# Three layers of a mixed model on one core: where the activations lie in SBUF, modulo 256 bytes

## The chip, the cores and the metric

The kernel runs on one core of one Trainium2 chip. The metric is the device time of one execution, in microseconds, first to last instruction with what lies around it; lower is better. Before the change it is 1613.02 us, the median of 3 runs.

## The reference

256 tokens of width 1024, float32, go through three layers. What matters here is that nearly all the work is products of the activations with large weight matrices, each weight used once:

```python
for layer in range(2):
    x = x + 0.5 * swiglu(rmsnorm(x, ffn1_norm[layer]), ffn1_w_gu[layer], ffn1_w_down[layer])   # 1024 -> 2 x 2816 -> 1024
    h = rmsnorm(x, mix_norm[layer])
    y = gated_deltanet(h, ...) if layer == 0 else sliding_window_attention(h, ...)
    x = x + y
    x = x + 0.5 * swiglu(rmsnorm(x, ffn2_norm[layer]), ffn2_w_gu[layer], ffn2_w_down[layer])
x = rmsnorm(x, final_norm)
# second block: one layer
proj = rms_norm(x, norm_mix) @ w_in             # attention, RWKV-7 in both directions, and gates
merged = gates_0 * (attn @ w_up_attn) + gates_1 * (rw @ w_up_rwkv)
x = x + merged @ w_out
x = x + square(relu(rms_norm(x, norm_ffn) @ w_ff1)) @ w_ff2          # 1024 -> 4096 -> 1024
x = x + (p @ w_ple) * sigmoid(rms_norm(x, norm_ple) @ w_ple_gate)
```

## The kernel before

**Weights.** All weights are cut into 225 pieces of 128 partitions by 2048 float32 (8192 bytes in each partition, 1 MB in all). There are four slots (`SLOTS`). SyncE loads piece p into `raw` with two transfers of 512 KB as soon as TensorE has used piece p - 4 (semaphore `piece_used`, L2380 to L2394). ScalarE rounds it to `w_hi` in the 32-bit matmul type F32R (L2715), VectorE writes the rest, `raw - w_hi`, over it as `w_lo` (L2888). `lo_ready` then releases the matmuls of the piece.

**Dense matmuls.** Activations are held transposed and split in the same way (`h_hi`/`h_lo` behind a norm, `g_hi`/`g_lo` behind a gate, and so on). `three()` (L2516) makes each product out of three matmuls, hi by hi, lo by hi and hi by lo; its lines are L2518, L2519 and L2520. In each the weight block of 128 x 128 is the stationary operand (a weight load, 512 bytes in each partition) and 256 tokens of the activation are the moving one (1024 bytes). Narrow jobs (L2523 on) run over chunks of 512 output columns and read `h`; wide jobs (L2572 on) run over the inner dimension and read `g`, `o`, `ao`, `mg`, `rw` or `p`. A piece is 16 such products, 48 matmuls. TensorE's queue is these in a fixed order; where a stage begins it waits for `h_ready`, which VectorE gives with `h_lo` (L2963).

**The gate logits.** In the first mixer, L637 to L639 do the same three matmuls 8 times over with `ba_hi`/`ba_lo` as weights. These are not in a slot but lie behind `h`.

**Addresses.** `Map.take` lays one tile behind the other and rounds each to 32 bytes. The map `fixed` begins at byte 16512 of each partition. The starts that matter, with their remainder modulo 256:

| tiles | start | modulo 256 |
|---|---|---|
| `w_hi`, `raw`/`w_lo` (four slots of 8192 each) | 16512, 49280 | 128 |
| `xT`, `cst` | 82048, 90240 | 128 |
| `p_hi`, `p_lo`, `sq`, `rstd`, `full3` | from 102464 | 64 |
| `h_hi`, `h_lo` | 122688, 130880 | 64 |
| the arena behind: `g_hi`, `g_lo`, `ba_hi`, `ba_lo`, `o_hi`, `ao_hi_b`, `mg_hi`, `rw_hi` and their partners | from 139072 | 64 |

Blocks of weights are 512 bytes apart and rows of activations 1024, so every operand of a dense matmul has the remainder of its tile. `y_tok`, the output, is laid from the end of SBUF down.

Of the kernel before, what the change touches and what calls it, by code (L numbers as in the profile page):

```python
# [195 lines left out]
def build(nc, A, out, stop=None):  # L196
    base = -(-16481 // 32) * 32
    fixed = Map(nc, base, 229344)
# [14 lines left out]
    sq = fixed.take("sq", [P, KD, T])  # L213
    rstd = fixed.take("rstd", [P, T])
    full3 = fixed.take("full3", [P, 3, 2, T])
    h_at = fixed.at
    h_hi = fixed.take("h_hi", [P, KD, T], F32R)
    h_lo = fixed.take("h_lo", [P, KD, T], F32R)
# [2900 lines left out]
```

## Time and profile before

| | us |
|---|---|
| median of 3 runs | 1613.02 |
| lowest, highest | 1601.33, 1614.93 |
| the profiled execution | 1607.01 |
| its span | 1605.0 |
| TensorE busy in it | 1536.2 (96%) |
| VectorE, ScalarE, GpSimd busy | 1064.6, 730.3, 69.9 |
| mean granted clock of TensorE | 0.989 |

All times of the trace are from this one execution, and sums are made against its 1607.01. The start-to-start distance of two matmuls that follow each other is shorter than the duration that the profile gives for one, since they overlap; where the text speaks of a beat it means that distance. The granted clock is a share of 2.4 GHz; it is 1.00 or 0.50.

### The profile page before, as it was taken

The page shows a single profiled execution, that of the slowest core. Times are in us where ns is not written, and L with a number is a line of the kernel's source. Part 1 is how long each engine was busy: PE and PEld are TensorE (multiplying, and loading weights), DVE is VectorE, ACT ScalarE, POOL GpSimd, SP SyncE. Part 2 cuts the span into 40 slices and gives each one's busy share as a digit, 9 for nine tenths or more (in the row PEclk, how much of TensorE's full clock was granted, in tenths as well). Part 3 has the DMA queues.
Part 4 walks back from the last instruction along what each step waited for, and adds up shares of the span by engine and source line. Part 5 has one row for each costly group of instructions (what it writes and reads, how often), then busy time and mean ns, then how long its engine had stood idle before and what let it go on. Part 6 is the DMA issues. An engine that isn't in the chain of part 4 may idle for free. (4 is left out here: it accounts for less than half of the span.)

```text
span 1605.0 us, 36127 instructions
## 1 busy us (share of the span) xinstructions
PE 1536.2 (96%) x15669; PEld 1478.2 (92%) x15669; DVE 1064.6 (66%) x1277; ACT 730.3 (46%) x814; POOL 69.9 (4%) x52
## 2 busy tenths in 40 slices
PE   7999989999999999999998999999997889999998
PEld 6999989878999999999988999999886778999997
DVE  5766487764867547664677766467768776777436
ACT  5443345543534344433446433354565444555333
POOL 2000000100100001000101000021000000100000
PEclk9999999999999999999999999999999999999999
DMA  8665545201556556555533555564320012555552
GB/s 269 189 192 201 185 157 169 96 2 51 183 188 193 200 184 184 183 184 187 181 131 96 182 187 191 185 201 145 120 79 3 3 56 81 184 184 189 202 186 79
DMA packets 155065, 243.26 MB, mean 152 GB/s; under 512 B 9283, under 2 KB 106174, under 8 KB 154814
## 3 DMA queue, kind: packets, MB, share of 16 engines
q1 hardware_dynamic: 154510, 240.63, 45.7%
q8 instruction: 102, 1.67, 0.4%
q10 hardware_dynamic: 432, 0.79, 0.2%
q14 instruction: 21, 0.17, 0.0%
HBM read 240.34 MB, written 1.05 MB: 150 GB/s over the span
## 5 line engine op out<-in xcount | busy, mean ns | idle before, releaser
L2888 DVE TENSOR_TENSOR w_lo<-raw,w_hi 128x2048 fp32r<-128x2048 f32 x225 | 522.9, 2335 | 243.0 <-ACT w_hi L2715 242.1
L2518 PE MATMUL dense_ps<-h_hi,w_hi 128*128 128x256 f32 x2368 | 668.3, 282 | 12.2 <-DVE h_lo L2963 8.6
L2519 PE MATMUL dense_ps<-h_lo,w_hi 128*128 128x256 f32 x2368 | 662.0, 280 | 0.0
L2520 PE MATMUL dense_ps<-h_hi,w_lo 128*128 128x256 f32 x2368 | 662.0, 280 | 0.0
L2715 ACT ACTIVATE w_hi<-raw 128x2048 fp32r<-128x2048 f32 x225 | 428.5, 1913 | 332.6 <-DMA raw<-in_ffn_w_down 116.2
L2518 PEld LDWEIGHTS dense_ps<-h_hi,w_hi 128*128 128x128 f32 x2368 | 450.5, 190 | 18.3 <-issue 17.8
L2519 PEld LDWEIGHTS dense_ps<-h_lo,w_hi 128*128 128x128 f32 x2368 | 447.4, 189 | 0.8 <-issue 0.5
L2520 PEld LDWEIGHTS dense_ps<-h_hi,w_lo 128*128 128x128 f32 x2368 | 448.1, 189 | 0.0
L2520 PE MATMUL dense_ps<-g_hi,w_lo 128*128 128x256 f32 x960 | 266.9, 278 | 0.0
L2518 PE MATMUL dense_ps<-g_hi,w_hi 128*128 128x256 f32 x960 | 266.9, 278 | 0.0
L2519 PE MATMUL dense_ps<-g_lo,w_hi 128*128 128x256 f32 x960 | 266.9, 278 | 0.0
L2518 PEld LDWEIGHTS dense_ps<-g_hi,w_hi 128*128 128x128 f32 x960 | 181.7, 189 | 0.0
L2520 PEld LDWEIGHTS dense_ps<-g_hi,w_lo 128*128 128x128 f32 x960 | 180.2, 188 | 0.0
L2519 PEld LDWEIGHTS dense_ps<-g_lo,w_hi 128*128 128x128 f32 x960 | 180.2, 188 | 0.0
L2843 ACT ACTIVATE act<-act 128x512 f32<-128x512 f32 x44 | 27.8, 632 | 178.4 <-DVE act L3055 178.4
L3055 DVE TENSOR_TENSOR act<-dense_ps,rstd 128x512 f32<-128x512 f32 x44 | 30.4, 691 | 58.2 <-PE dense_ps L2520 54.7
L2683 POOL TENSOR_TENSOR sq<-sq 128x512 f32<-128x512 f32 x14 | 20.1, 1438 | 924.0 <-ACT sq L2786 924.0
L2954 DVE TENSOR_TENSOR g_lo<-full,g_hi 128x512 f32 (+1 forms) x60 | 41.5, 692 | 4.9
L595 ACT ACTIVATE ly_r<-mixer_ps 128x512 f32<-128x512 f32 x48 | 26.5, 594 | 23.7 <-PE mixer_ps L538 18.0
L3059 DVE TENSOR_TENSOR full<-act,full 128x512 f32<-128x512 f32 x44 | 31.5, 716 | 8.7 <-ACT act L2843 4.8
L3006 DVE SCALAR_TENSOR_TENSOR xT<-dense_ps,xT 128x1024 f32<-128x1024 f32 x14 | 17.1, 1221 | 30.2 <-PE dense_ps L2520 30.2
L981 DVE SCALAR_TENSOR_TENSOR qkv<-dense_ps,cols,qkv 128x255 f32<-128x255 f32 (+2 forms) x72 | 29.7, 475 | 11.1 <-ACT qkv L836 10.7
(554 smaller groups left out, 1750.5 us busy)
## 6 DMA issues: line engine op xcount, KB each, us to landing
raw<-in_ffn_w_gu SPq DMA_DIRECT2D x176, 512.0 KB, 4.6
raw<-in_ffn_w_down SPq DMA_DIRECT2D x88, 512.0 KB, 4.1
raw<-in_w_ff SPq DMA_DIRECT2D x64, 512.0 KB, 4.2
raw<-in_w_in SPq DMA_DIRECT2D x36, 512.0 KB, 4.4
raw<-in_a_w_in SPq DMA_DIRECT2D x32, 512.0 KB, 4.3
raw<-in_a_w_out SPq DMA_DIRECT2D x8, 512.0 KB, 4.0
raw<-in_b_w_in SPq DMA_DIRECT2D x8, 512.0 KB, 4.2
raw<-in_b_w_out SPq DMA_DIRECT2D x8, 512.0 KB, 4.1
```

What stands on the lines that cost most here:

```text
L595: act.activation(y[:, 4 * half:4 * half + 4, :], bank_pair(half), ACT.Copy).then_inc(y_kept, 1)
L981: last = dve.scalar_tensor_tensor(out=o_, in0=ps, scalar=cols[:, at_:at_ + 1], in1=o_, op0=ALU.mult, op1=ALU.add)
L2518: pe.matmul(o, hi, mh, start=start, stop=False)
L2519: pe.matmul(o, hi, ml, start=False, stop=False)
L2520: return pe.matmul(o, lo, mh, start=False, stop=stop)
L2683: pool.tensor_tensor(src[:, k:k + 2, :], src[:, k:k + 2, :], src[:, k + 2:k + 4, :], ALU.add).then_inc(sq_folded, 1)
L2715: act.activation(w_hi[:, p % SLOTS, :], raw[:, p % SLOTS, :], ACT.Copy).then_inc(hi_ready, 1)
L2843: act.activation(act2[:, q, :, :], act2[:, q, :, :], ACT.Silu).then_inc(act_ready, 1)
L2888: dve.tensor_tensor(w_lo[:, p % SLOTS, :], raw[:, p % SLOTS, :], w_hi[:, p % SLOTS, :].bitcast(F32), ALU.subtract).then_inc(lo_ready, 1)
L2954: return dve.tensor_tensor(lo, full, hi.bitcast(F32), ALU.subtract)
L3055: dve.tensor_tensor(act2[:, q, :, :], lower, by_rms(2), ALU.mult).then_inc(gate_scaled, 1)
L3059: link(dve.tensor_tensor(full2[:, q, :, :], act2[:, q, :, :], full2[:, q, :, :], ALU.mult))
```

## The change

In front of `h_hi` 192 bytes are left free. `h_hi` and `h_lo` begin at 122880 and 131072 then, the arena at 139264; all of them have the remainder 0 modulo 256, the weight slots still 128. The tiles ahead of `h_hi` stay, and so does `y_tok`. All else is the same.

```diff
     rstd = fixed.take("rstd", [P, T])
     full3 = fixed.take("full3", [P, 3, 2, T])
+    fixed.at += 192
     h_at = fixed.at
     h_hi = fixed.take("h_hi", [P, KD, T], F32R)
     h_lo = fixed.take("h_lo", [P, KD, T], F32R)
     arena = fixed.at
```

## Rows read from the trace of the kernel before

**Rows 1.** The page, part 1: busy us, share of the span and instructions

```profile
PE 1536.2 (96%) x15669; PEld 1478.2 (92%) x15669; DVE 1064.6 (66%) x1277; ACT 730.3 (46%) x814; POOL 69.9 (4%) x52
```

**Rows 2.** The page, part 5: line, form and count, busy and mean, idle before

```profile
L2888 DVE TENSOR_TENSOR w_lo<-raw,w_hi 128x2048 fp32r<-128x2048 f32 x225 | 522.9, 2335 | 243.0 <-ACT w_hi L2715 242.1
L2518 PE MATMUL dense_ps<-h_hi,w_hi 128*128 128x256 f32 x2368 | 668.3, 282 | 12.2 <-DVE h_lo L2963 8.6
...
L2715 ACT ACTIVATE w_hi<-raw 128x2048 fp32r<-128x2048 f32 x225 | 428.5, 1913 | 332.6 <-DMA raw<-in_ffn_w_down 116.2
```

**Rows 3.** Table of stretches: width, each engine's busy us (count), clock, DMA

```profile
41.00:198.00 157.00, 157.00 (x1388) 157.00 (x1387) 99.44 (x86) 61.01 (x40) 0.00 (x0) 1.00 0.59 193
427.00:594.00 167.00, 167.00 (x1476) 167.00 (x1475) 103.25 (x87) 67.18 (x46) 0.00 (x0) 1.00 0.60 195
1402.00:1566.00 164.00, 164.00 (x1449) 164.00 (x1449) 96.59 (x80) 77.42 (x65) 0.00 (x0) 1.00 0.56 193
597.00:783.00 186.00, 186.00 (x1579) 185.90 (x1577) 114.81 (x95) 76.99 (x58) 6.29 (x4) 1.00 0.58 186
886.00:1060.00 174.00, 174.00 (x1479) 174.00 (x1479) 103.47 (x87) 67.65 (x47) 0.00 (x0) 1.00 0.58 187
```

**Rows 4.** Groups by line, TensorE and its weight loads, 427 to 594 us

```profile
L2518 PE MATMUL dense_ps<-h_hi,w_hi 128*128 128x256 f32 x318 | 87.8, 276 | 0.0
...
L2518 PEld LDWEIGHTS dense_ps<-h_hi,w_hi 128*128 128x128 f32 x317 | 59.5, 188 | 0.0
```

**Rows 5.** The same groups, 597 to 783 us

```profile
L2519 PE MATMUL dense_ps<-h_lo,w_hi 128*128 128x256 f32 x349 | 98.1, 281 | 0.0
...
L2518 PEld LDWEIGHTS dense_ps<-h_hi,w_hi 128*128 128x128 f32 x348 | 66.7, 192 | 0.0
```

**Rows 6.** Timeline of TensorE: start us, us, instruction, idle before it

```profile
595.59 0.36 PE L2518 MATMUL dense_ps<-h_hi,w_hi 128*128 128x256 f32 x1 [0.63 <-DVE h_lo L2963]
595.78 0.28 PE L2519 MATMUL dense_ps<-h_lo,w_hi 128*128 128x256 f32 x1
...
596.49 0.28 PE L2519 MATMUL dense_ps<-h_lo,w_hi 128*128 128x256 f32 x1
```

**Rows 7.** The same timeline, up to the first gate logit, and the last

```profile
240.97 0.28 PE L2519 MATMUL dense_ps<-h_lo,w_hi 128*128 128x256 f32 x1
...
241.54 0.28 PE L637 MATMUL mixer_ps<-h_hi,ba_hi 128*128 128x256 f32 x1
...
244.30 0.28 PE L639 MATMUL mixer_ps<-h_hi,ba_lo 128*128 128x256 f32 x1
```

**Rows 8.** The tile `mixer_ps`, 241 to 245 us: durations ns min/median/max, first and last start

```profile
L637 PEld LDWEIGHTS mixer_ps<-h_hi,ba_hi x8: 188/192/192, 241.4 to 243.9; 128*128 128x128 f32 x8
L637 PE MATMUL mixer_ps<-h_hi,ba_hi x8: 283/283/284, 241.5 to 244.1; 128*128 128x256 f32 x8
```

**Rows 9.** Line L2519 in 198 to 427 us and in 1060 to 1200 us

```profile
L2519 PE MATMUL dense_ps<-h_lo,w_hi x291: 275/276/420, 207.3 to 427.0; 128*128 128x256 f32 x146
...
L2519 PE MATMUL dense_ps<-h_lo,w_hi x288: 276/281/416, 1061.5 to 1198.9; 128*128 128x256 f32 x144
```

**Rows 10.** Table of stretches, 16 to 19 us

```profile
16.00:19.00 3.00, 3.00 (x16) 3.00 (x15) 2.68 (x3) 3.00 (x7) 0.00 (x0) 0.50 1.11 350
```

**Rows 11.** Timeline of TensorE there, first and last of six

```profile
16.92 0.41 PE L2518 MATMUL dense_ps<-h_hi,w_hi 128*128 128x256 f32 x1
...
17.99 0.41 PE L2520 MATMUL dense_ps<-h_hi,w_lo 128*128 128x256 f32 x1
```

**Rows 12.** Timeline of TensorE, eight matmuls of `ones` by `sq`

```profile
199.20 1.89 PE L2627 MATMUL mixer_ps<-sq,cst 128*128 128x256 f32 x8
```

**Rows 13.** Timeline of the weight loads behind the pause of rows 6

```profile
595.56 0.19 PEld L2518 LDWEIGHTS dense_ps<-h_hi,w_hi 128*128 128x128 f32 x1 [0.80 <-issue]
595.67 0.19 PEld L2519 LDWEIGHTS dense_ps<-h_lo,w_hi 128*128 128x128 f32 x1
```

**Rows 14.** The page, part 6: transfers, KB each, median us to landing

```profile
raw<-in_ffn_w_gu SPq DMA_DIRECT2D x176, 512.0 KB, 4.6
```

## The prediction

> **What bounds the kernel now.** I read the page first. Its table of busy times gives TensorE 96% of the span, VectorE 66% and ScalarE 46% [rows 1]. The costliest groups are the three lines of `three()` and the splits that feed them [rows 2]. So the rate of the dense matmuls sets the time, if they run without gaps. The table of stretches says so: in five long stretches TensorE and its weight loads are busy all the time, at a granted clock of 1.00 (2.4 GHz), VectorE about 60% of it [rows 3].
>
> The same table holds the point of this case. A window counts every matmul that touches it, and one lasts 276 or 281 ns, so some 2.4 of each count began before the window. From 427 to 594 us that is 1476 - 2.4 in 167 us, a beat (start to start) of 113.3 ns; from 886 to 1060 us it is 1479 - 2.4 in 174 us, a beat of 117.8 ns [rows 3]. Code, shapes, tiles and clock are the same in both; only the job differs. Line by line, a matmul of the first stretch lasts 276 ns and its weight load 188 ns [rows 4]; in the second they last 281 ns, and one of the three loads 192 ns [rows 5]. I call them the short and the long beat.
>
> The timeline shows that a beat is kept while the stream runs and chosen anew where it restarts. The short beat of [rows 4] ends where TensorE waits 0.63 us for `h_lo`; from 595.78 on it runs at 118 ns (0.71 us for six) [rows 6].
>
> Does the place in SBUF matter to it? The reader should look for dense matmuls whose operands lie otherwise. In all 10,800 dense matmuls (225 pieces, one split of L2888 each [rows 2], of 48) the weight piece begins 64 bytes above the moving tile, modulo 256 (128 against 64). There is one exception of the same form: the 24 matmuls of `gate_logits` (L637 to L639), where `ba_hi`/`ba_lo` and `h_hi`/`h_lo` all lie at 64, a distance of 0. They start at 241.54 without a pause, out of a stream in the short beat (0.57 us for the five beats before), and go from there to 244.30 in 23 beats, 120.0 ns each [rows 7]. Each lasts 283 ns, and nearly each of their loads 192 ns [rows 8]. So three beats are seen: 120.0 at distance 0, and 113.3 or 117.8 at distance 64.
>
> **What the change does.** No instruction, wait, transfer or byte is added or removed. `h_hi` and all behind it move up 192 bytes, from 64 to 0 modulo 256; weight slots, `xT`, constants, `sq`, `rstd`, `full3` and `p_hi`/`p_lo` stay. For 10,752 of the 10,800 dense matmuls (all but the 48 of `ple`, which read `p_hi`/`p_lo`) the distance goes from 64 to 128. The 24 of `gate_logits` keep distance 0.
>
> **What each part costs.** *The mix of beats now.* The three stretches in the short beat hold 1388 + 1476 + 1449 = 4,313 matmuls, the two in the long one 1579 + 1479 = 3,058 [rows 3]. The other 3,430 lie in stretches where both occur. In these the median of L2519 is 276 ns from 198 to 427 us and 281 ns from 1060 to 1200 us [rows 9], so I take half of each. That makes 4,770 in the long beat and 5,980 of the moved ones in the short.
>
> *If distance 128 always gives the short beat*, 4,770 x 4.5 ns = 21.5 us go.
>
> *The other bounds.* Distance 128 has no row in a stream of this form, so I take the nearest from both sides. Above: the long beat everywhere costs 5,980 x 4.5 = 27 us; the 120.0 ns of distance 0 costs 5,980 x 6.7 + 4,770 x 2.2 = 51 us. Below: at the granted clock of 0.50 (1.2 GHz) [rows 10] the same matmuls take 1.07 us for five beats, 214 ns each, so 107 ns at 2.4 GHz is the stream alone [rows 11]. Eight matmuls of `ones` by `sq`, which take two such passes each, start (1.89 - 0.38)/7 = 215.7 ns apart, 2.4 more than twice 106.7 [rows 12]. So no beat should be below some 109 ns; 10,752 x 4.1 = 44 us under the short beat. A load is near that too: 595.56 to 595.67, 110 ns, for two loads before the stream has formed [rows 13]. I take the short beat: it is a steady state that rows show, and the load leaves little below it.
>
> *Does the rest keep up?* A piece is 48 matmuls, 5.44 us in the short beat. In the short stretch from 427 to 594 us VectorE is busy for 103.25 of 167 us and ScalarE for 67.18; TensorE has no gap at all [rows 3]. A freed slot is refilled in 4.6 us [rows 14], then split in 1.9 by ScalarE and 2.3 by VectorE [rows 2], 8.8 in all, against 16.3 us that the three other pieces last. Of the two states the faster is already fed, so a saved beat is saved time; at the floor below VectorE's share would go from 62% to 64%.
>
> *Other accesses that move against each other.* The small matmuls of the mixers also read moved against unmoved tiles, but most restart every few instructions and wait for VectorE or ScalarE. VectorE's `h_lo` reads `xT` and `h_hi`, whose distance changes too; TensorE waits 8.6 us for it in all [rows 2], and if it slowed by as much as the beats differ, 4%, that is 0.3 us. Both at nothing, up to 2 us either way for the range.
>
> **Sum.** The profiled execution took 1607.0 us (span 1605.0 and 2.0 around it). 1607.0 - 21.5 = 1585.5. The median of the runs is 1613.0, six above it, and they spread from 1601 to 1615. I hold the choice at restarts for the cause of that spread: 6 us are 1,300 beats of 4.5 ns. A kernel with one beat would not have it, so I add nothing.
>
> A rule speaks against all of this. The Trainium skill ("SBUF — State Buffer", section Who interferes with whom) says that TensorE and ScalarE never wait on anyone, and "TensorE: Matmul & The Clock Gate", Step-by-step: what each phase is for, that the two read ports are independent, so loading the next weights takes no bandwidth from the running matmul. By these the distance is nothing, and the time stays 1607. The rows of `gate_logits` speak against it, as one place of 24 matmuls, which also differ in adding to one PSUM tile all along.
>
> **The rivals.**
> - *The distance decides nothing, or both beats remain.* For it: the beat is a matter of how the stream restarts, and distance 64 already gives both. The moving operand reads 1024 bytes in a beat and the weights 512, so it laps them twice in a ring of 256 whatever the distance; the change only moves the places from 1/8 and 5/8 of a beat to 1/4 and 3/4. Against: the switch at 241.54 without a pause. Time: 1607, and by the runs 1601 to 1615.
> - *The other side: the long beat always.* If a catch further inside a beat is what can't be absorbed, every restart falls into it. It decides by its share: with 4,770 + 6/0.0045 = 6,100 of the 10,752 in the long beat (57%) the kernel stands at the median of 1613, and from 9,700 (90%) it is slower by over 1%. Time: 1607 + 27 = 1634.
> - *As bad as distance 0*, if what matters is a ring of 128 bytes: 128 is then 0. For it: one row shows 0 to be bad, and none shows how long the ring is. Time: 1607 + 51 = 1658.
> - *Better than the short beat*: the 6.6 ns that it has above the stream alone are themselves a collision that the new distance avoids. Time down to 1585 - 44 = 1541. Against: the load's 110 ns.
>
> **How the numbers follow.** Distance 0 costs most and 64 less; 128 is the farthest in a ring of 256, so the short beat is likeliest: 0.45, 1585 us, its own range 1575 to 1595. Better than it 0.08; no effect or both beats 0.24; the long beat 0.13; as distance 0 0.10. The range 1560 to 1640 leaves out 0.10 above and most of 0.08 below. A measurement here can tell about 1% of 1613 from no change: faster (under 1597) 0.45 + 0.08 = 0.53, within 0.24, slower 0.13 + 0.10 = 0.23.
>
> **What would show it.** Right: in the table of stretches every long stretch at 113.3 ns; L2518 to L2520 at 276 ns and loads at 188 in all jobs; 24 matmuls of `gate_logits` still 283 ns; no new gap of TensorE. Wrong: 281 ns and 192 ns where 276 and 188 stood; or a duration that is none of these; or `gate_logits` changed though its distance isn't. If the beat shortens and the span doesn't, TensorE must show waits for `w_lo`, and the paragraph on keeping up was wrong.

## The result and the profile after

The kernel got slower. The median of four runs is 1643.1 us (1640.6 to 1644.2), beside it that of the kernel before 1607.2 us (1601.0 to 1614.9). The ratio is 1.0219, with a 95% interval of 1.0159 to 1.0278. The forecast was 1585, its range 1560 to 1640.

The profiled execution took 1642.43 us (span 1640.5), 35.4 more than that of before. First the page of the kernel after, busy times and costliest groups (all lines stand one further down than before):

```profile
PE 1571.0 (96%) x15669; PEld 1513.3 (92%) x15669; DVE 1064.4 (65%) x1277; ACT 730.0 (44%) x814; POOL 69.7 (4%) x52
...
L2519 PE MATMUL dense_ps<-h_hi,w_hi 128*128 128x256 f32 x2368 | 676.6, 286 | 11.4 <-DVE h_lo L2964 7.8
L2889 DVE TENSOR_TENSOR w_lo<-raw,w_hi 128x2048 fp32r<-128x2048 f32 x225 | 522.3, 2332 | 249.8 <-ACT w_hi L2716 248.9
```

TensorE is busy 34.8 us longer than before with the same 15669 matmuls, and VectorE and ScalarE as long as before [rows 1]. The wait for `h_lo` went from 8.6 to 7.8 us and the mean `w_lo` split from 2335 to 2332 ns [rows 2]. So nothing else got slower and no wait was added: the matmuls themselves come later after each other. The table of stretches shows it, three long ones of the kernel after (columns as in [rows 3]):

```profile
43.00:205.00 162.00, 162.00 (x1367) 162.00 (x1366) 96.78 (x84) 60.65 (x39) 0.00 (x0) 1.00 0.59 186
440.00:600.00 160.00, 160.00 (x1350) 160.00 (x1350) 98.10 (x82) 60.74 (x40) 0.00 (x0) 1.00 0.57 183
625.00:800.00 175.00, 175.00 (x1474) 174.90 (x1473) 104.26 (x86) 67.25 (x45) 0.32 (x1) 1.00 0.57 182
```

Counted as in the prediction, 1350 - 2.4 in 160 us is a beat of 118.7 ns, and the other two come to 118.7 and 118.9. It is neither of the two beats of [rows 3]: 5.4 ns above the short one and 0.9 above the long one, at the same granted clock of 1.00. The groups by line of the kernel after, 440 to 600 us, give the durations:

```profile
L2521 PE MATMUL dense_ps<-h_hi,w_lo 128*128 128x256 f32 x313 | 88.1, 281 | 0.0
...
L2519 PEld LDWEIGHTS dense_ps<-h_hi,w_hi 128*128 128x128 f32 x312 | 58.7, 188 | 0.0
```

All three lines last 281 ns, and all loads 188, where [rows 4] had 276 and 188 and [rows 5] 281 and, for one load in three, 192. Taken over all dense matmuls and gate logits whose start follows the last one by 90 to 130 ns (10,635 before, 10,619 after), the mean distance of starts is 115.41 ns before and 118.71 after. (118.71 - 115.41) x 10,752 = 35.5 us, against 35.4 measured. Nor does the work of the other engines make the beat: from 450 to 540 us of the kernel after, matmuls that start while VectorE and ScalarE are both busy follow at 118.64 ns, those that start while both are idle at 118.64 too.

Distance 128 has a second beat, which the long stretches don't show. Some 440 of the moved matmuls, in four streams, follow each other at 120.0 ns. The longest of these streams begins at 220.6 us, behind a stretch at a granted clock of 0.50 (214 to 220 us), and runs up to the gate logits. Its end, 24 beats in 2.88 us:

```profile
248.83 0.28 PE L2521 MATMUL dense_ps<-h_hi,w_lo 128*128 128x256 f32 x1
...
251.71 0.28 PE L2521 MATMUL dense_ps<-h_hi,w_lo 128*128 128x256 f32 x1
251.83 0.28 PE L638 MATMUL mixer_ps<-h_hi,ba_hi 128*128 128x256 f32 x1
```

It weighs little, 440 x 1.3 ns = 0.6 us in the whole time.

A control lies in the same execution. The 48 matmuls of `ple` read `p_hi`/`p_lo`, which did not move. Timeline of TensorE in the kernel after, inside that piece:

```profile
1599.81 0.28 PE L2520 MATMUL mixer_ps<-p_lo,w_hi 128*128 128x256 f32 x1
...
1601.62 0.28 PE L2521 MATMUL mixer_ps<-p_hi,w_lo 128*128 128x256 f32 x1
```

Sixteen beats in 1.81 us, 113 ns: the short beat, in the one place where the distance is still 64. The other 24 matmuls of `ple`, behind 16 of another form, beat at 117.8, the other beat of that distance. The gate logits, whose distance stayed 0 although both their operands moved, last 283 ns as before [rows 8], in the tile `mixer_ps` of the kernel after, 246 to 254 us:

```profile
L638 PE MATMUL mixer_ps<-h_hi,ba_hi x7: 281/283/283, 251.8 to 254.0; 128*128 128x256 f32 x7
```

They are unchanged, as they should be, but they prove less: the stream ahead of them has the same 120.0 ns here.

### The profile page after: what moved, and what is told of

It is laid out like the page before. It is cut to its first block and busy times, and to the rows that moved or that the text cites. A ratio compares the mean times of both kernels' runs of the same rounds, so it can differ in the third digit from the quotient of the medians.

```text
span 1640.5 us, 36127 instructions
## 1 busy us (share of the span) xinstructions
PE 1571.0 (96%) x15669; PEld 1513.3 (92%) x15669; DVE 1064.4 (65%) x1277; ACT 730.0 (44%) x814; POOL 69.7 (4%) x52
## 5 line engine op out<-in xcount | busy, mean ns | idle before, releaser
L2519 PE MATMUL dense_ps<-h_hi,w_hi 128*128 128x256 f32 x2368 | 676.6, 286 | 11.4 <-DVE h_lo L2964 7.8
L2889 DVE TENSOR_TENSOR w_lo<-raw,w_hi 128x2048 fp32r<-128x2048 f32 x225 | 522.3, 2332 | 249.8 <-ACT w_hi L2716 248.9
L2521 PE MATMUL dense_ps<-h_hi,w_lo 128*128 128x256 f32 x2368 | 669.7, 283 | 0.0
L2520 PE MATMUL dense_ps<-h_lo,w_hi 128*128 128x256 f32 x2368 | 669.7, 283 | 0.0
L2519 PEld LDWEIGHTS dense_ps<-h_hi,w_hi 128*128 128x128 f32 x2368 | 449.6, 190 | 17.5 <-issue 17.0
L2520 PEld LDWEIGHTS dense_ps<-h_lo,w_hi 128*128 128x128 f32 x2368 | 449.7, 190 | 0.9 <-issue 0.5
L2521 PEld LDWEIGHTS dense_ps<-h_hi,w_lo 128*128 128x128 f32 x2368 | 449.2, 190 | 0.0
L2520 PE MATMUL dense_ps<-g_lo,w_hi 128*128 128x256 f32 x960 | 270.1, 281 | 0.0
L2519 PE MATMUL dense_ps<-g_hi,w_hi 128*128 128x256 f32 x960 | 270.1, 281 | 0.0
L2521 PE MATMUL dense_ps<-g_hi,w_lo 128*128 128x256 f32 x960 | 270.1, 281 | 0.0
L2520 PEld LDWEIGHTS dense_ps<-g_lo,w_hi 128*128 128x128 f32 x960 | 180.7, 188 | 0.0
L2519 PEld LDWEIGHTS dense_ps<-g_hi,w_hi 128*128 128x128 f32 x960 | 180.7, 188 | 0.0
L2521 PEld LDWEIGHTS dense_ps<-g_hi,w_lo 128*128 128x128 f32 x960 | 180.7, 188 | 0.0
```

The lines of the kernel that those rows point to most:

```text
L2519: pe.matmul(o, hi, mh, start=start, stop=False)
L2520: pe.matmul(o, hi, ml, start=False, stop=False)
L2521: return pe.matmul(o, lo, mh, start=False, stop=stop)
L2889: dve.tensor_tensor(w_lo[:, p % SLOTS, :], raw[:, p % SLOTS, :], w_hi[:, p % SLOTS, :].bitcast(F32), ALU.subtract).then_inc(lo_ready, 1)
```

## The experiments

Every kernel below computes the same with the same instructions; only places in SBUF differ. "Mean beat" is the mean distance of starts defined above, from the one profiled execution. The kernel before ran beside each group, too: 1602.8 us (median of 13) beside the e1 kernels, 1601.0 beside e2, 1605.6 beside e3, 1604.6 beside e4 and 1598.5 beside e5. A single run of a kernel at distance 64 is uncertain by 10 us either way (the 13 runs went from 1593.2 to 1613.2), so the readings of single runs rest on beats.

The theories that the expectations call A and B are: A, the beat depends on the distance between weight piece and moving tile, modulo 256; B, on where the activations themselves lie.

### Distance or place

`e1_both_moved` puts the activations where the kernel after has them, at 0 modulo 256, and takes the weights along, so that the distance is 64 again:

```diff
-    base = -(-16481 // 32) * 32
+    base = -(-16481 // 32) * 32 + 192
```

> The 192 bytes stand in front of the weight slots instead, so that weights, constants and activations all move together: the activations lie at 0 modulo 256 as in the changed kernel, but the weights 64 above them as before. Theory A: both beats of before, 113.3 and 117.8 ns, 1600 to 1615 us, and no beat of 118.7. Theory B (the activations at 0 modulo 256 are slow by themselves): 118.7 ns in all jobs, about 1643 us.

1604.1 us, median of 10 (1591.9 to 1613.2), ratio 1.0012 (0.9979 to 1.0046). In its profiled execution (1591.9) the mean beat is 114.04. Its stretch from 450 to 560 us:

```profile
450.00:560.00 110.00, 110.00 (x973) 110.00 (x972) 72.11 (x64) 43.67 (x29) 0.00 (x0) 1.00 0.59 196
```

973 - 2.4 in 110 us is the short beat, 113.3 ns; other jobs of the same execution run at 117.8. Both beats of before are back with the activations at the place of after. The distance theory holds and the place theory falls.

`e1_distance_0` and `e1_distance_192` leave the weights and use the gap of the change with another size, `fixed.at += 64` and `fixed.at += 128` in place of 192:

> The gap is 64 bytes: h_hi and all behind it lie at 128 modulo 256, as the weight pieces. Theory A: the dense matmuls do as the 24 of the gate logits did at distance 0, 120.0 ns a beat and 283 ns a matmul everywhere, 10,752 x (120.0 - 115.4) = 49 us over before, about 1656 us. Theory B: as before, 1600 to 1615.

> The gap is 128 bytes in place of 192: h_hi and all behind it lie at 192 modulo 256, the weight pieces 192 above them (or 64 below). Theory A (the beat of the dense matmuls hangs on the distance from the moving tile to the weight piece modulo 256, and on nothing else that the gap moves): one or two steady beats that no other distance has; if only the size of the distance on the ring counts, 192 is as 64, both 113.3 and 117.8 ns, about 1600 to 1615 us; if it counts which of the two is ahead, something else between 109 ns (1541 us) and 120 ns (1657 us). Theory B (the absolute place of the activations modulo 256 decides, 0 being bad): beats as before, 113.3 and 117.8.

Distance 0: 1650.8 us, mean beat 119.93. The page of that kernel, and its stretch from 450 to 560 us:

```profile
L2519 PE MATMUL dense_ps<-g_hi,w_hi 128*128 128x256 f32 x960 | 271.7, 283 | 0.0
```

```profile
450.00:560.00 110.00, 110.00 (x919) 110.00 (x918) 73.08 (x69) 41.63 (x29) 0.00 (x0) 1.00 0.55 182
```

919 - 2.4 in 110 us is 120.0 ns, and 283 ns is what the gate logits take [rows 7, 8]. The reading of 24 matmuls that the prediction leant on holds for the moved 10,752 as well: every unbroken stream of 60 or more beats at 119.8 to 120.0.

Distance 192: 1629.3 us, median of 4 (1628.7 to 1629.5), ratio 1.0170 (1.0113 to 1.0227), mean beat 117.68. Its stretches:

```profile
450.00:560.00 110.00, 110.00 (x936) 110.00 (x936) 72.23 (x66) 43.02 (x29) 0.00 (x0) 1.00 0.57 185
...
920.00:1060.00 140.00, 140.00 (x1191) 140.00 (x1190) 83.78 (x71) 52.63 (x34) 0.00 (x0) 1.00 0.55 185
```

Both are the long beat, 117.8. So a kernel that has almost only the long beat exists (its last job alone, some 190 matmuls, runs at 113.3), and its time is near what the prediction gave for that rival, 1634. Its four runs lie within 0.8 us, where the 13 beside them of the kernel before spread over 20. That fits the prediction's statement that the spread at distance 64 is the choice between the two beats.

### Half of the change

`e1_arena_only` leaves `h_hi`/`h_lo` at distance 64 and moves only what lies behind them to 128:

```diff
     h_lo = fixed.take("h_lo", [P, KD, T], F32R)
+    fixed.at += 192
     arena = fixed.at
```

> The 192 bytes stand behind h_lo: h stays at distance 64, and only g, o, ao, mg, rw (3,648 of the dense matmuls) come to distance 128. Theory A: in one run the jobs that read h have beats of 113.3 or 117.8 ns (matmuls of 276 or 281 ns) and those that read the arena 118.7 (281.4 ns), with a switch at each job's border without a pause; 3,648 x (118.7 - 115.4) = 12 us, about 1619 us. Against it: the beat is chosen at a restart and kept, so g has what h had ahead of it.

1612.0 us, mean beat 116.09. The groups by line, 450 to 560 us, hold narrow and wide jobs side by side:

```profile
L2519 PE MATMUL dense_ps<-h_hi,w_hi 128*128 128x256 f32 x255 | 70.4, 276 | 0.0
...
L2519 PE MATMUL dense_ps<-g_hi,w_hi 128*128 128x256 f32 x67 | 18.9, 281 | 0.0
```

The same line, form and weight slots give 276 ns where `h` is read, not moved, and 281 where `g` is, moved. All wide jobs of the run beat at 118.7 and all narrow ones at 113.3 or 117.8. The cost goes exactly with the tiles that move.

### How the distances lie

With another gap in front of `h_hi` (32, 96, 160 and 224 bytes) come distances 32, 224, 160 and 96. `e2_far_128` takes a gap of 448, which is 128 modulo 256 like the change, but 384 and not 128 modulo 512.

> The gap is 32 bytes: the weight pieces lie 32 above the moving tiles. Theory A in the form 'the beat changes with each 64 bytes': 32 falls between 0 (120.0 ns) and 64 (113.3 or 117.8) and does as one of them, 1650 or 1590 to 1615 us. Theory A in the form 'the beat changes gradually': a beat of its own, about 117 to 119 ns, 1620 to 1640 us.

> The gap is 224 bytes: the weight pieces lie 96 above the moving tiles, between 64 (113.3 or 117.8 ns) and 128 (118.7). By steps of 64 it does as one of the two; gradually it has a beat of its own. If one beat of 113.3 exists that every restart falls into, it is here or at 32, and the time is 1585 us.

> The gap is 96 bytes: the weight pieces lie 224 above the moving tiles, between 192 (117.8 ns) and 256 = 0 (120.0). By steps of 64: 117.8 or 120.0, 1629 or 1651 us. Gradually: between the two, about 1640 us.

> The gap is 448 bytes, 256 more than in the changed kernel: the distance is again 128 modulo 256, but 384 modulo 512 where the changed kernel has 128. Theory A with a ring of 256: beats of 118.7 ns in all jobs and 1640 to 1645 us, as the changed kernel. With a ring of 512 or more: another beat, as 384 would be a distance not tried so far.

> The gap is 160 bytes, the last distance of the ring in steps of 32: weight pieces 160 above the moving tiles, between 128 (118.7 ns) and 192 (117.8). Theory A: a beat of about 118 ns and 1630 to 1643 us, and none of 113.3, which has stood at distance 64 only.

The four `e4` kernels go finer. Tiles begin at multiples of 32 bytes, so `h_hi` and `h_lo` are taken 8 columns longer and read from inside. The cut below is the line of `h_hi` for distance 48; that of `h_lo` and the gaps that keep the rest in place are left out, and starts of 2 or 6 columns and other gaps give the other distances. Only `h` is moved; the wide jobs stay at 64 as a control.

```diff
-    h_hi = fixed.take("h_hi", [P, KD, T], F32R)
+    h_hi = fixed.take("h_hi", [P, KD * T + 8], F32R)[:, 4:4 + KD * T].rearrange("p (k t) -> p k t", t=T)
```

> h_hi and h_lo lie 48 below the weight pieces, the arena 64 as before (narrow jobs show distance 48, wide jobs 64). If the short beat belongs to a band around 64: narrow jobs at 113.3 ns, alone or beside 117.8. If to the 64-byte step alone: about 118 as at 32.

> h_hi and h_lo lie 56 below the weight pieces, the arena 64. Band: 113.3 ns in the narrow jobs, alone or beside 117.8. Single place: about 118. If the long beat is missing here: narrow jobs all at 113.3, 1590 us or less.

> h_hi and h_lo lie 72 below the weight pieces, the arena 64. Band: 113.3 ns in the narrow jobs, alone or beside 117.8. Single place: 117.3 to 120.0 as at 96. If the long beat is missing here: narrow jobs all at 113.3, 1590 us or less.

> h_hi and h_lo lie 80 below the weight pieces, the arena 64. Band: 113.3 ns in the narrow jobs, alone or beside 117.8. Single place: 117.3 to 120.0 as at 96.

All together, in the order of the distance. The last column has the beats of the moved jobs, each a mean over a stream of at least 60 matmuls without a break; in the `e4` rows these are the narrow jobs, while the mean beat beside them is over all jobs.

| distance | us | mean beat | beats of the moved jobs, ns |
|---|---|---|---|
| 0 | 1650.8 | 119.93 | 120.0 |
| 32 | 1637.7 | 118.32 | 118.3 |
| 48, `h` alone | 1622.9 | 117.22 | 119.2; 116.7 for some 450 matmuls |
| 56, `h` alone | 1637.7 | 117.99 | 120.0 to 120.5 |
| 64, before | 1607.0 | 115.41 | 113.3 or 117.8 |
| 72, `h` alone | 1631.7 | 117.93 | 120.0 |
| 80, `h` alone | 1626.2 | 117.45 | 119.3 |
| 96 | 1641.5 | 118.70 | 117.3, 118.7 or 120.0 |
| 128, the change | 1642.4 | 118.71 | 118.7; 120.0 for some 440 matmuls |
| 128 (384 modulo 512) | 1640.1 | 118.69 | 118.7; 120.0 for some 260 |
| 160 | 1652.9 | 119.95 | 120.0 |
| 192 | 1628.7 | 117.68 | 117.8; 113.3 for some 190 |
| 224 | 1622.9 | 117.23 | 116.7 or 117.8 |

The beat is no smooth function of the distance. 64 is the best of the twelve, and its neighbours 8 bytes away are as bad as 0. The stretch from 450 to 540 us, all in `h`, first of `e4_distance_72`, then of `e3_distance_160`:

```profile
450.00:540.00 90.00, 90.00 (x752) 90.00 (x752) 59.13 (x54) 33.80 (x23) 0.00 (x0) 1.00 0.59 186
```

```profile
450.00:540.00 90.00, 90.00 (x753) 90.00 (x752) 58.65 (x56) 34.55 (x24) 0.00 (x0) 1.00 0.58 181
```

752 - 2.4 and 753 - 2.4 in 90 us are 120.1 and 119.9 ns. Several expectations missed. 160 was to lie between 128 and 192 and has the beat of 0; 224 was to have 117.8, 120.0 or something between and has 116.7 beside 117.8; no band around 64 was found, and without one 48 and 56 were to be about 118. The groups by line of `e4_distance_48`, 450 to 560 us:

```profile
L2521 PE MATMUL dense_ps<-h_hi,w_hi 128*128 128x256 f32 x270 | 76.3, 283 | 0.0
...
L2521 PE MATMUL dense_ps<-g_hi,w_hi 128*128 128x256 f32 x41 | 11.3, 276 | 0.0
```

The repeat at 384 modulo 512 has the beat of the change, from 450 to 560 us in `e2_far_128` (930 - 2.4 in 110 us, 118.6):

```profile
450.00:560.00 110.00, 110.00 (x930) 110.00 (x929) 74.28 (x68) 42.71 (x29) 0.00 (x0) 1.00 0.59 187
```

So at this distance 256 more bytes change nothing but which streams fall to 120.0. That fits a ring of 256 and speaks against one of 512. So does the kernel before: modulo 512 its weight pieces lie 320 bytes above `h`, but 64 above `p`, and both jobs show 113.3 and 117.8. A ring of 128 is excluded by 0 and 128, or 64 and 192, which differ.

In the `e4` kernels a second thing differs from 64: the tiles begin off a multiple of 64. Nor do the distances 32, 96, 160 and 224 keep them on one. Perhaps such a start costs by itself. `e5_all_moved_32` adds 32 to `base`, so that distance 64 stays and every tile begins at 32 modulo 64:

> 32 more bytes in front of the weight slots: all tiles move together, the distance stays 64, but weights (160 modulo 256) and activations (96) both begin 32 behind a multiple of 64. Theory A, distance alone: 113.3 and 117.8 ns as before, 1590 to 1615 us. Theory L (a start off the multiple of 64 costs by itself, as one more line to read): about 118 ns or more, 1630 us or more.

1610.5 us, mean beat 115.23, and only the beats 113.3 and 117.8 in it:

```profile
450.00:560.00 110.00, 110.00 (x973) 110.00 (x972) 74.49 (x66) 43.52 (x30) 0.00 (x0) 1.00 0.61 194
625.00:780.00 155.00, 155.00 (x1318) 155.00 (x1318) 92.87 (x78) 56.96 (x37) 0.00 (x0) 1.00 0.58 188
```

A start off a multiple of 64 costs nothing at distance 64. Starts at 8, 16 or 24 modulo 32 were not tried at that distance; for 48 to 80 this stays possible.

### Which pair of operands

While one matmul runs, the weights of the next are loaded, so two distances could count: that between the moving tile and its own weights, or that to the weights being loaded. In the change all are the same. Four kernels move one tile of the four that `three()` reads:

```diff
# e3_w_lo_128: 64 bytes before the slots of raw/w_lo, 192 behind them
+    fixed.at += 64
     raw_at = fixed.at
# e3_h_lo_128: 192 bytes before h_lo, 64 behind it (e3_h_lo_192: 128 and 128)
+    fixed.at += 192
     h_lo = fixed.take("h_lo", [P, KD, T], F32R)
# e5_w_hi_128: base + 64, and 192 bytes between w_hi and raw
+    fixed.at += 192
     raw_at = fixed.at
```

> Only raw/w_lo moves, by 64 bytes: w_lo lies 128 above the moving tiles, w_hi 64 as before. Each dense product is h_hi by w_hi (L2518 of before), h_lo by w_hi (L2519), h_hi by w_lo (L2520), and the profile starts the load of the next matmul within 4 ns of the start of this one. Theory C (the moving operand of a matmul meets the load that runs beside it, the next one's): w_lo is loaded beside L2519, so L2519 alone is stretched. Theory O (a matmul is slowed by the place of its own weights): L2520 alone. Both: a mean beat between 113.3 and 118.7 ns, about 115 to 117, 1600 to 1625 us. Theory N (all three must agree, the mix falls in a state of its own): another beat.

> Only h_lo moves: it lies 128 below the weight pieces, h_hi and the arena 64 as before. It is the moving operand of L2519, beside which w_lo is loaded. Theories C and O both: in narrow jobs L2519 stretched as in e3_w_lo_128 by theory C, a mean beat of some 115 to 117 ns; in wide jobs 113.3 or 117.8 as before; 1600 to 1620 us. If C holds, its narrow jobs have the same pattern of beats as those of e3_w_lo_128; if O, another.

> Only h_lo moves, to distance 192; h_hi and the arena stay at 64. Theory C or O: L2519 as at distance 192, the other two as at 64, a mean beat of the narrow jobs of 115 to 118 ns (1605 to 1630 us). A mix that leaves the long beat no hold would give 113.3 always, 1585 us.

> Only w_hi moves: it lies 128 above the moving tiles, raw/w_lo 64 as before. w_hi is loaded beside L2518 and L2520 of before (2 of 3), w_lo beside L2519. Theory C (each matmul by the load beside it) or O (by its own weights): two of three matmuls as at 128, one as at 64, a mean beat no lower than that of e3_w_lo_128, 118.2, and no higher than 118.7. Theory N (the sequence as a whole falls in a steady state of its own): another beat, lower or higher than both.

| kernel | us | mean beat | beats of streams of 60 or more, ns |
|---|---|---|---|
| `w_lo` at 128 | 1633.2 | 118.23 | 118.2 or 118.3 in every job |
| `h_lo` at 128 | 1628.5 | 117.25 | narrow 118.7 to 119.0; wide 113.3 or 117.8 |
| `h_lo` at 192 | 1628.5 | 117.14 | narrow 117.8; wide both |
| `w_hi` at 128 | 1635.0 | 118.17 | 117.8, 118.7 or 120.0, by job |

If each matmul paid for its own pair, `w_lo` or `h_lo` at 128 would put one matmul in three at 118.7 and leave two at 113.3, a mean of 115.1. Measured are 118.2 and more. The page of `e3_w_lo_128`:

```profile
L2520 PE MATMUL dense_ps<-h_hi,w_hi 128*128 128x256 f32 x2368 | 676.2, 286 | 11.4 <-DVE h_lo L2965 7.9
...
L2521 PE MATMUL dense_ps<-h_lo,w_hi 128*128 128x256 f32 x2368 | 667.9, 282 | 0.0
L2522 PE MATMUL dense_ps<-h_hi,w_lo 128*128 128x256 f32 x2368 | 663.0, 280 | 0.0
```

In this kernel only L2522 has moved weights, and it is the shortest of the three. One matmul out of place shifts all three: from 450 to 540 us the starts of L2521, L2522 and L2520 follow those before them by 119.0, 119.5 and 116.2 ns, and none by 113.3. Both pairings put one matmul in three at 128 in the first two kernels and so ask for like results; the patterns differ, and no line is the dear one in all of them. By either pairing `w_hi` at 128 was to have a mean beat between 118.2 and 118.7. The mean, 118.17, lies at the edge of that, but its streams don't: most beat at 117.8 and some at 120.0. That rather fits the third theory of the expectations (N), by which the sequence as a whole falls into a state of its own. The runs settle neither pairing. They do show that a sum by parts is wrong, and that moving a third of the pairs costs most of what moving all of them costs (2.8 of the 3.3 ns for `w_lo`).

## Why the prediction was wrong

**What it had right.** What bounds the kernel, and that nothing else limits it: the time follows the beat. 1607.0 + (mean beat - 115.41) x 10,752 gives the time of every profiled execution within 6 us (distance 0: 1655.6 against 1650.8; `e1_both_moved`: 1592.3 against 1591.9). The mechanism: the distance modulo 256, not the place; the job and the restart choose only among the beats of a distance. The reading of the gate logits as a price of distance 0 was right: 120.0 ns there, 120.0 in `e1_distance_0`. "Does the rest keep up" and "other accesses at nothing" held, though a slower beat tests the first only weakly; `e1_both_moved` tests it better, with most jobs at 113.3 and 1591.9 us. The count of matmuls in the long beat was too low: with 4,770 of them there the mean would be 113.3 + 4.5 x 4,770 / 10,750 = 115.3, and it is 115.4, some 260 more, 1 us.

**The step that failed** is "I take the short beat" under *The other bounds*, and its ground in the last part: "Distance 0 costs most and 64 less; 128 is the farthest in a ring of 256". Two points, one good and one bad, were made into a slope. The runs show no slope: 8 bytes from the good place a beat is 6.7 ns longer (with the start of the tile as a second suspect), and 160 costs as much as 0. The 113.3 ns were taken for the ordinary state of the stream, to which a farther distance would return. They are the exception: usual at 64, and elsewhere held only at 192, by the last job. The term "4,770 x 4.5 = 21.5 us gained" should have been 5,980 x 5.4 + 4,770 x 0.9 = 36.6 us lost, which the profiled run gives as 35.4.

**The rivals.** "The long beat always" had the right sign and the nearest time, 1634 of 1643. It was priced with a beat of before, because only two were known for distance 64; 128 has one of its own, 0.9 ns longer, and 0.9 x 10,752 = 9.7 us accounts for the 9 us that it misses. "As bad as distance 0" (1658) falls for 96% of the moved matmuls, 118.7 not being 120.0; the some 440 others have that very beat. "No effect" falls by the result itself (1.0159 to 1.0278) and by distance 192 (1.0113 to 1.0227). "Better than the short beat" has no run for it at all: no distance gave a beat under 113.3.

**The rule of the skill.** By the Trainium skill, "SBUF — State Buffer", Who interferes with whom, TensorE never waits on anyone, and by its "TensorE: Matmul & The Clock Gate", Step-by-step: what each phase is for, loading the next weights takes no read bandwidth from the running matmul. From this the prediction drew that the place would cost nothing. The measurement decides against that reading: moved by 192 bytes, the same matmuls take 35 us longer, and moved together with their weights, nothing. That it is the two reads that meet is an argument from this dependence; no row shows the ports. Here the prediction weighed rule and row rightly, and then took from the row a size and a sign for another distance, which it couldn't give.

**The range** ended at 1640, three below the result. It left out 0.10 above, for a beat of 120.0, and put all that lay between the long beat and that one to nothing, though nothing in the rows forbade values between.

**What stays open.** Why 64 and 128 have two beats each and what picks one where the stream restarts; which pair of operands meets; whether 48, 56, 72 and 80 suffer from the distance or from a start off a multiple of 32. No kernel faster than the one before was found. By an estimate, making its stream keep the short beat everywhere would give 1607.0 - (115.41 - 113.3) x 10,752 = 1584 us, which no run reached (the nearest is 1591.9).

## What to carry to other kernels

Where a long stream of matmuls is the bound, treat the distance modulo 256 between weights and moving tile as a setting to be measured, in steps of 32 bytes, and keep it fixed when a tile is added or resized: an innocent 192 bytes in front of a tile cost 2.2% here. Two measured distances say nothing of a third. Read the beat (starts per stretch) by tile; a tile that kept its distance, in the same execution, is the control that tells the cause.

## What the runs showed of the hardware

- At a granted clock of 1.00 a stream of 128x256 matmuls in F32R, each with its own 128x128 weights, has beats of 113.3, 116.7, 117.3, 117.8, 118.2 to 118.3, 118.7, 119.2 to 119.3 and 120.0 to 120.5 ns. Only the places of the operands differ between the kernels, and 120.0 is 6% over 113.3.
- At one distance the beat can take several values: 113.3 or 117.8 at 64; 117.3, 118.7 or 120.0 at 96; 118.7 or 120.0 at 128. One is held while the stream runs, and another can follow where it restarts, or behind matmuls at another distance: the 24 gate logits stand between 113.3 and 117.8 in the kernel before, and between 120.0 and 118.7 in the one after. Four runs of the kernel at 192 lie within 1 us and four at 128 within 4, while 13 at 64 spread over 20.
- One tile out of place among the four slows all three matmuls of a product, not only its own: 118.2 ns against 115.1 for a sum by parts.
